# Latent heads in pairs on two column halves, differential scores as three fp32r products, and a unit's maximum ahead of the last unit's scaling

## What is computed

```python
def _softmax_attention(q, k, v, scale):          # layer 0: 8 heads, 64+32 wide keys, 64 wide values
    s = jnp.einsum('bhqd,bhkd->bhqk', qb, k).astype(jnp.float32) * scale
    p = jax.nn.softmax(s, axis=-1)
    return jnp.einsum('bhqk,bhkd->bhqd', p.astype(v.dtype), v)

def _diff_attention(q1, q2, k1, k2, v, lam, scale):   # layer 1: 8 heads, two 64 wide halves, 128 wide values
    p1 = jax.nn.softmax(jnp.einsum('bhqd,bhkd->bhqk', qa, k1).astype(jnp.float32) * scale, axis=-1)
    p2 = jax.nn.softmax(jnp.einsum('bhqd,bhkd->bhqk', qb, k2).astype(jnp.float32) * scale, axis=-1)
    return jnp.einsum('bhqk,bhkd->bhqd', (p1 - lam * p2).astype(v.dtype), v)
```

## Time and profile before

| | |
|---|---|
| median of 3 timed runs | 1863.83 us (1862.94 to 1865.37) |
| the profiled execution: its time, its span | 1864.37 us, 1862.6 us |
| busy share of the span | TensorE 81%, VectorE 40%, ScalarE 23%, GpSimd 11% |
| mean granted TensorE clock | 0.913 of full speed |

### The profile page before, as it was taken

The page is one execution under the profiler, slowest core; times in us unless marked ns, Lnnn a source line. Parts: engine busy times, 40 slices in busy tenths (PEclk is TensorE's granted clock), DMA queues, the critical chain, the costliest instruction groups (busy, mean ns, idle before and its releaser), DMA issues. The chain is left out here.

```text
span 1862.6 us, 25715 instructions
## 1 busy us (share of the span) xinstructions
PE 1517.4 (81%) x9767; PEld 1213.7 (65%) x9768; DVE 744.2 (40%) x1388; ACT 426.4 (23%) x832; POOL 214.2 (11%) x166
## 2 busy tenths in 40 slices
PE   4699999656899997599993199989997867999970
PEld 1588888555576444477882199987884446777760
DVE  0312122266477343311114835428993752111118
ACT  1311212242343011011112312125552111101113
POOL 1000000112000032100003400010000321100016
PEclk9899999878999998699997599999998977999995
DMA  7576755701000901559994032220006225877763
GB/s 270 176 238 211 242 182 160 171 12 31 1 1 1 296 34 54 170 173 342 354 352 168 23 94 69 80 60 1 1 1 183 102 91 198 280 260 256 269 215 146
DMA packets 190509, 277.82 MB, mean 149 GB/s; under 512 B 12888, under 2 KB 130352, under 8 KB 190416
## 3 DMA queue, kind: packets, MB, share of 16 engines
q1 hardware_dynamic: 180032, 239.15, 39.0%
q0 software_dynamic: 9520, 34.24, 5.3%
q10 hardware_dynamic: 864, 3.15, 0.4%
HBM read 246.90 MB, written 34.85 MB: 151 GB/s over the span
## 5 line engine op out<-in xcount | busy, mean ns | idle before, releaser
L480 PEld LDWEIGHTS psum<-in_parts 128*128 128x128 f32 x3360 | 411.3, 191 | 59.2 <-issue 59.2
L480 PE MATMUL psum<-in_parts 128*128 128x258 f32 (+1 forms) x3360 | 421.2, 286 | 25.3 <-PEq L322 25.3
L773 PE MATMUL psum<-layer 128*128 128x512 f32 x400 | 173.7, 594 | 2.7 <-PEq L698 2.7
L1777 PEld LDWEIGHTS psum<-layer 128*128 128x128 f32 x1280 | 145.7, 192 | 15.2 <-issue 7.6
L1777 PE MATMUL psum<-layer 128*128 128x128 f32 x1280 | 146.5, 275 | 6.7 <-DVE layer L1983 6.7
L1777 PEld LDWEIGHTS psum<-layer,arena 128*128 128x128 f32 x1152 | 137.9, 200 | 13.2 <-issue 6.7
L1777 PE MATMUL psum<-layer,arena 128*128 128x128 f32 x1152 | 138.6, 284 | 5.3 <-DVE layer L1983 3.6
L773 PEld LDWEIGHTS psum<-layer 128*128 128x128 f32 x400 | 75.8, 191 | 95.2 <-issue 95.2
L566 DVE COPY arena<-psum 128x258 f32<-128x258 f32 (+1 forms) x70 | 29.7, 425 | 240.8 <-PE psum L480 240.8
L1168 PE MATMUL psum<-layer 128*128 128x320 f32 (+1 forms) x384 | 114.2, 434 | 5.0 <-PEq L1358 1.7
L1265 ACT ACTIVATE layer<-psum,layer 128x640 f32<-128x640 f32 (+1 forms) x120 | 84.3, 705 | 118.5 <-DVE layer L1211 118.5
(11 more groups left out here) (298 smaller groups left out, 1872.7 us busy)
## 6 DMA issues: line engine op xcount, KB each, us to landing
arena<-in_moe_w SPq DMA_DIRECT2D x48, 1024.0 KB, 9.3
layer<-in_moe_w SPq DMA_DIRECT2D x48, 1024.0 KB, 8.7
in<-in_ada_w SPq DMA_DIRECT2D x40, 1024.0 KB, 5.2
y_rows<-layer SPq DMA_DIRECT2D x64, 256.0 KB, 8.5
in<-in_ev_w_in SPq DMA_DIRECT2D x15, 1032.0 KB, 7.6
in<-in_od_w_in SPq DMA_DIRECT2D x11, 1024.0 KB, 5.1
start<-in_ada_w SPq DMA_DIRECT2D x8, 1024.0 KB, 16.6
arena<-mod_rows SPq DMA_DIRECT2D x16, 512.0 KB, 7.7
```

The lines of the kernel that those rows point to most:

```text
L480: last = T.matmul(bank(g % W_BANKS)[:, 0:cw], a, b[:, k], start=(k == 0 and m == 0), stop=(k == KD - 1 and m == 2))
L773: last = T.matmul(bank(g % 4), feats[k][:, t * P:(t + 1) * P], wout[:, k, j * BANK:(j + 1) * BANK], start=(k == 0), stop=(k == kt - 1))
L1777: last = T.matmul(dst[:, (2 * f + m) * P:(2 * f + m + 1) * P], weights[m][:, k, f * P:(f + 1) * P], xT[:, k, :], start=(k == 0), stop=(k = ...
```

## The change

`heads_attention` is replaced by two functions. In both VectorE takes `top(u)` ahead of `mix(u - 1)`; the order of TensorE's and ScalarE's steps stays.

- `latent_heads`: `values` is done for two heads at once, in every second turn: for each of the five key tiles a product for the even head into PSUM rows 0 to 63 and one for the odd head into rows 64 to 127. The result of both is copied out at once. The transposed weights have four buffers for two. VectorE now copies two of the five transposed tiles, ScalarE three.
- `difference_heads`: each of the four fp32 score matmuls becomes three fp32r products over 64 rows of contraction, without the zero padding. ScalarE copies all five transposed tiles.
- `differential_attention`: the evacuation of every query and key item is done twice, ScalarE writing the rounded part and VectorE the remainder (of the PSUM value and the rounded part); the zero padding falls away.
- Buffers move (`MLA_OUT`, the heads' buffers behind the projection), and the upper part of SBUF is taken anew around the differential attention; GpSimd drains at the end of retention.

```diff
+        def latent_heads(units, qT, kT, value, e_buf, put, rsum, nmax, pT):
...
+            LONG, ND = sum(len(kt) > 1 for kt in tiles), 2
+            def pair_at(u):
+                return u % 2 == 1 and u >= 3
...
+                @block.tensor
...
+                    def values(p):
+                        pe.wait_ge(c_d, 2 * p + 2)
+                        pe.wait_ge(c_a, min(2 * p + 2, LONG))
+                        if p >= 2:
+                            pe.wait_ge(put_s, p - 1)
+                        out = bank(6 + p % 2)
+                        for n, kt in enumerate(tiles[2 * p]):
+                            for r in range(2):
+                                u = 2 * p + r
+                                last = T.matmul(out[MDV * r:MDV * (r + 1), 0:P], value(units[u][1], kt), pT[:, u % 4, n, :],
+                                                start=(n == 0), stop=(n == len(tiles[u]) - 1))
+                        last.then_inc(valued, 1)
+
+                    for u in range(U + 2):
+                        if u < U:
+                            score(u)
+                        if pair_at(u):
+                            values((u - 3) // 2)
+                        if 1 <= u <= U:
+                            turn(u - 1)
...
+                @block.vector
...
+                    for u in range(U + 2):
+                        if u < U:
+                            top(u)
+                        if 1 <= u <= U:
+                            mix(u - 1)
+                        if pair_at(u):
+                            out((u - 3) // 2)
+                        if 1 <= u <= U:
+                            copy_p(u - 1)
...
+        def difference_heads(units, qT, kT, value, e_buf, lamr, put, rsum, nmax, pT, squares):
...
+            PRODUCTS = ((0, 0), (0, 1), (1, 0))
...
+                    def score(u):
+                        t, h = units[u]
+                        for s in range(2):
+                            if u:
+                                pe.wait_ge(expd, 2 * u - 1 + s)
+                            for a in range(1 if t == 0 else 2):
+                                for m, (x, y) in enumerate(PRODUCTS):
+                                    out, k0, n = (view(s, 1), NT * P, P) if t == 0 else (view(s, NT)[:, a], a * HK, HK)
+                                    last = T.matmul(out, qT(t, h, s, x), kT(h, s, y, k0, n), start=(m == 0), stop=(m == 2))
+                            last.then_inc(scored, 1)
...
                 @block.vector
...
                     for u in range(U + 2):
+                        if u < U:
+                            top(u)
                         if 1 <= u <= U:
                             mix(u - 1)
-                        if u < U:
-                            top(u)
                         if u >= 2:
                             out(u - 2)
-                        if 1 <= u <= U:
-                            copy_p(u - 1)
...
+                        A.copy(pT[:, u % 2, 0:n], bank(4, 2)[:, 0:n * P].rearrange("p (n q) -> p n q", n=n)).then_inc(copied, 1)
...
         def differential_attention(pj):
-                    evac(dve, 1)
+                    for n, (kind, h) in enumerate(items):
+                        dve.wait_ge(ev_a, n + 1)
+                        src = bank(2 * (n % 4), 2)
+                        if kind == "k":
+                            V.tensor_tensor(kT[1][:, h, :], src[:, 0:NK * P], whole(kT[0][:, h, :]), ALU.subtract).then_inc(ev_d, 1)
+                        else:
+                            V.scalar_tensor_tensor(qT[1][:, h, :], src[:, 0:TOK], DIFF_SCALE, whole(qT[0][:, h, :]),
+                                                   ALU.mult, ALU.subtract).then_inc(ev_d, 1)
...
-                    evac(act, 0)
+                    for n, (kind, h) in enumerate(items):
+                        act.wait_ge(tr, n + 1)
+                        src = bank(2 * (n % 4), 2)
+                        if kind == "k":
+                            A.copy(kT[0][:, h, :], src[:, 0:NK * P]).then_inc(ev_a, 1)
+                        else:
+                            A.mul(qT[0][:, h, :], src[:, 0:TOK], DIFF_SCALE).then_inc(ev_a, 1)
```

More of the change, by code:

```diff
@@ L1124, in _ @@
                         norm(t)
[L1126 to L1134, removed]
+        def latent_heads(units, qT, kT, value, e_buf, put, rsum, nmax, pT):
+            scored, maxed, expd = sem("mla_scored"), sem("mla_maxed"), sem("mla_expd")
+            mixed = sem("mla_mixed")
+            turned, c_a, c_d, valued, put_s = (sem(f"mla_{n}") for n in ("turned", "ca", "cd", "valued", "put"))
             U = len(units)
             tiles = [[NT] if t == 0 else list(range(NT)) for t, _ in units]
+            LONG, ND = sum(len(kt) > 1 for kt in tiles), 2
             def view(b, nk):
@@ L1157, in score @@
                         t, h = units[u]
[L1158 to L1169, removed]
+                        if u >= 2:
+                            pe.wait_ge(expd, u - 1)
+                        if t == 0:
+                            T.matmul(view(u % 2, 1), qT(t, h), kT(h, NT * P, P), start=True, stop=True).then_inc(scored, 1)
+                        else:
+                            for a in range(2):
+                                last = T.matmul(view(u % 2, NT)[:, a], qT(t, h), kT(h, a * KEYS // 2, KEYS // 2), start=True, stop=True)
+                            last.then_inc(scored, 1)
                     def turn(u):
@@ L1218, in mix @@
                         dchain.join(dve)
[L1219 to L1228, removed]
@@ L1237, in out @@
+                        e1, e2 = weights(u, 0, nk), weights(u, 1, nk)
+                        V.scalar_tensor_tensor(e1, e2, r[:, 1:2], e1, ALU.mult, ALU.add).then_inc(mixed, 1)
                     def out(u):
                         dve.wait_ge(valued, u + 1)
[L1239 to L1242, removed]
+                        V.tensor_scalar(put(*units[u]), out_of(u), rsum[:, 1, 2 * u:2 * u + 1], None, ALU.mult).then_inc(put_s, 1)
@@ L1467, in differential_attention @@
             lam1 = small[:, 32:34]
[L1468 to L1481, removed]
-                        if who == 0:
-                            last = A.mul(dst, half, DIFF_SCALE)
-                        else:
-                            last = V.tensor_scalar(dst, half, DIFF_SCALE, None, ALU.mult)
-                    last.then_inc(done, 1)
+            items = [("q", h) for h in range(DH)] + [("k", h) for h in range(DH)]
             with nc.Block(no_gpsimd_drain=True) as block:
@@ L1497, in _ @@
                           pj[:, 0, 2 * D:3 * D].rearrange("p (h d) -> p h d", h=DH))
-                items = [("q", h) for h in range(DH)] + [("k", h) for h in range(DH)]
-                @block.gpsimd
-                def _(pool):
-                    for r in range(2):
-                        rows = slice(DDH * (1 - r), DDH * (2 - r))
-                        nc.gpsimd.memset(qT[rows, :, r, :], 0.0)
-                    pool.drain()
                 @block.vector
```

188 lines of the change are left out of this document (124 added, 64 removed).

## The result

The changed kernel takes 1918.32 us (median of 4, 1916.03 to 1921.55), the kernel before beside it 1864.07 us (median of 4, 1862.94 to 1865.37): 1.0293 times as long, 95% interval 1.0278 to 1.0308. The profiled executions have spans of 1918.5 and 1862.6 us, 55.9 us apart.

| stretch | before, us | after, us | difference |
|---|---|---|---|
| start to the last block of retention's scores | 437.8 | 435.3 | -2.5 |
| from there to the latent preparation | 19.8 | 23.4 | +3.6 |
| latent preparation | 38.1 | 38.8 | +0.7 |
| latent loop, to the output projection | 111.3 | 129.2 | +17.9 |
| to layer 1, and layer 1 to the differential stage | 640.4 | 639.2 | -1.1 |

What follows compares the result with a forecast made beforehand. TensorE was taken to bound both loops before the change. Latent +12.3, differential +27.9, evacuation +2.7 and short units +2 sum to +44.9 us on 1864.37, so 1909 us; range 1890 to 1934.

Steps and rivals of the forecast that it cites:

- The ring: Both loops: scores, maximum, scaling, transposes, next scores run one after another; latent 3.42 us against 3.01, differential 4.75 against 3.82.
- the second half's maximum: Differential turn: starts 2.00 us after the scores start, after all twelve products; the first half's lies under the second half's products.
- my 0.15 us apart: Differential scores: pitch of the twelve fp32r products of 320 columns, taken in proportion to columns; 0.12 us otherwise.
- my 0.09: Differential turn: gap in us between transposes and next scores, for 64 rows of contraction; bounds 0 and 0.17.
- Rival B: Latent values: the column halves don't overlap, the pair takes 2.48 us; +12.6, 1922 us; chance 0.12.
- Rival C: Differential scores: weight loads show in the 64-row form, 0.32 us a product; +61, 1970 us; chance 0.09.
- Rival E: Both loops: the ring doesn't close and TensorE's work is the bound, differential 3.45 us, latent 2.39; 1837 us; chance 0.08.
- Rival D: Both loops: the clock falls because TensorE now idles in each turn; chance 0.05.
- Short units: Short units of both loops: the same ring on one key tile, +2 us together, bounds 0 and +8.
- The drain after retention: End of retention: costs nothing, because the barrier there waits for VectorE anyway.
- Evacuation: Ahead of the differential loop: ScalarE and VectorE each handle all 16 items; +2.7 us, bounds +1.6 and +3.7.

Runs made afterwards that it cites:

- experiment 1: The changed kernel with VectorE's order put back in both loops, scaling of the last unit before the maximum: 1857.19 us, 0.9968 of the kernel before.
- experiment 2: The kernel before with only VectorE's order changed, the maximum ahead of the last unit's scaling: 1914.62 us, 1.0281 of the kernel before.
- experiment 5: The changed kernel with transposes, copies, values and outputs one turn later and a third buffer for the weights: 1843.16 us, 0.9898 of the kernel before.
- experiment 4: The changed kernel with both halves' score products on rows 0 to 63: 1956.15 us in one execution, with other tokens sent to the experts.
- experiment 3: The kernel before with one GpSimd drain added at the end of retention: 1864.39 us, 1.0009 of the kernel before.
- experiment 6: The kernel of experiment 5 with 24 unread transposes on TensorE ahead of the differential loop: 1845.71 us, 0.9913 of the kernel before.
- experiment 7: The kernel of experiment 5 with the latent loop's paired values and their output one turn later still: 1831.47 us, 0.9841 of the kernel before.

## Why the prediction was right, and where it was off

The forecast was 1909 us and the kernel takes 1918: slower, for the reason given, with +55.9 us of span against +44.9.

**The ring: right.** The latent period is 3.43 us (3.42 forecast), the differential one 4.73 (4.75). By periods the rings cost 30 x 0.42 + 30 x 0.91 = 39.9 us, against 40.2 forecast. Experiments 1 and 2 show the order to be the cause from both sides: taken out of the changed kernel the loss is gone, put into the old one it is there. Experiment 5 shows that it is the ring and not the order as such, for there VectorE has the new order and TensorE no longer stands behind it.

**Inside the differential turn two terms were off and cancelled; that they left the sum within 0.02 us is luck.** I let the second half's maximum start 2.00 us after the scores. The first starts after 1.18 us, and the two, back to back, are what the reciprocal stands behind: 2.65 us where I had 2.73. So it is not the twelfth product that sets this step but VectorE's second maximum, queued behind its first. The twelve products are faster than my 0.15 us apart because the two row halves overlap: twelve take 1.54 us on both halves and, in experiment 4, 2.02 us on one. There they come (2.02 - 0.16) / 12 = 0.155 us apart, so the rate taken from the earlier trace rows was right and the overlap was missing. From the transposes to the scores it is 0.69 us, not 0.64: a gap of 0.14, between my 0.09 and my upper bound of 0.17. The runs show how long the gap is and not what causes it.

**Rivals B and C: fallen.** Twenty value records on both column halves take 1.31 us, as ten on one half did, and TensorE still waits 0.33 us after them. Twelve products with twelve weight loads take 1.54 us, not 12 x 0.32 = 3.84: the loads are hidden, on one row half too (2.02 us in experiment 4). **Rival E: fallen for the changed kernel,** and my bound for it, 3.45 us a differential unit once the ring is open, needs more than the old order: experiment 1 has that order and gets 3.80, where VectorE and ScalarE form the next ring. The bound holds where the transposes move (3.34 us, experiment 5).

**The terms that were too small** make up the 11 us:
- *The clock at the loops' starts, for which the sum had nothing.* Rival D had it fall through both loops, for TensorE's idle time. Inside them it stays at 1.00, with TensorE idle for 28% and 25% of the time. It fell at their starts: before, the first units of both run at full speed, at 1.00 from 495 to 505 and from 1258 to 1280 us; after, the granted clock is 0.50 from about 500 to 513 and 1288 to 1301 us. TensorE after, at both places:

```profile
503.19 2.34 PE L1162 MATMUL psum<-layer 96*128 96x320 f32 x4
...
508.24 2.34 PE L1162 MATMUL psum<-layer 96*128 96x320 f32 x4
```
```profile
1289.57 2.74 PE L1300 MATMUL psum<-heads_parts 64*128 64x320 f32 x12 [1.21 <-ACT arena L1374]
...
1295.74 2.67 PE L1300 MATMUL psum<-heads_parts 64*128 64x320 f32 x12
```

  A latent turn takes 5.05 us there (503.19 to 508.24) in place of 3.43: the ring has TensorE's scores and transposes in it, and both take about twice as long (the scores 2.34 us for 1.24; from the transposes to the next scores it is 1.12 us, 502.07 to 503.19, for 0.61). The long units grew by 16.6 and 30.3 us; less the rings' 12.6 and 27.3 this leaves 4.0 and 3.0 us, **7.0 us** for the starts. That all of it is the clock is not separated: the second differential turn (6.17 us for 4.11) may hold some of the ring as well. At the latent start the low clock need not be the change's doing, for experiment 3, whose latent loop is the old one, has it too:

```profile
500.00:502.00 2.00, 1.51 (x7) 1.28 (x7) 1.36 (x3) 0.57 (x1) 0.00 (x0) 0.50 0.00 0
```

  There it comes in some kernels (experiments 1 to 4 and 6, and the changed kernel) and not in others (before, experiments 5 and 7). At the differential start, in one profiled execution of each, it falls in every kernel with the new products and evacuation (the changed one, experiments 1 and 4 to 7) and in none with the old ones; experiment 2, with the new order, keeps 1.00 there from 1278 to 1300 us. So the order alone does not bring it down. What does is open.
- *Short units:* +1.3 and +3.4, **4.7 us** where I had 2. A differential one takes 2.6 us at 0.50 (1448.42 to 1451.02) and 2.1 at full clock (1444.12 to 1446.22), against 1.885 before.
- *The drain after retention:* costed at nothing because the barrier waits for VectorE anyway. It does not wait for VectorE alone: **2.4 us**, by the rows of experiment 3 (VectorE idle 2.88 us at the barrier for 0.51).
- *Evacuation:* **+3.4** for +2.7. VectorE's steps after, in order:

```profile
1271.75 3.81 DVE L1610 SCALAR_TENSOR_TENSOR heads_parts<-psum,heads_parts 128x640 fp32r<-128x640 f32 x5 [0.86 <-ACT heads_parts L1628]
1275.80 0.82 DVE L1610 SCALAR_TENSOR_TENSOR heads_parts<-psum,heads_parts 128x640 fp32r<-128x640 f32 x1 [0.24 <-ACT heads_parts L1628]
...
1278.92 7.00 DVE L1608 TENSOR_TENSOR heads_parts<-psum,heads_parts 128x768 fp32r<-128x768 f32 x8 [0.16 <-ACT heads_parts L1626]
```

  Its own steps are a little cheaper than taken (0.76 us apart for 640 columns, 0.87 for 768, in place of 0.80 and 0.92). What I left out are four waits for ScalarE behind the first, 0.16 to 0.24 us each, and a later start: VectorE's first step comes 5.82 us after the first transposes (at 1265.93), where the forecast has 5.53 (1247.37 to 1252.90).

These four are 12.8 us more than I had. The rings are 0.3 less, and the preparation's +0.7 and the small differences elsewhere (-2.5, -1.1, +0.2, and +1.2 beside the drain) take off 1.5, which leaves the 11 us.

## What to carry to other kernels

Before an engine's order is changed, follow the waits of one turn through every engine's own program order: where the first instruction of a turn on one engine waits for the last of the same turn on another, that chain is the period, however idle the engines are, and a faster operation outside it gives nothing. Move the consumers along with the producer: the order with which the changed kernel lost 2.9% goes with a gain of 1.0% once transposes, copies and values come a turn later (experiment 5), and of 1.6% with the paired values later still (experiment 7). When one ring is opened, look for the next, here 3.80 us between VectorE and ScalarE, before promising the engine's own work as the bound.

## What the runs showed of the hardware that was not expected

- Products that contract over 64 rows overlap with those on the other 64 rows, though all six of one half were issued ahead of the other six: twelve of 320 columns in 1.54 us, against 2.02 us on the same rows (experiment 4).
- Two column halves at once cost next to nothing: twenty value records in the 1.31 us of ten.
- TensorE's granted clock can stay at 0.50 for some 13 us of a loop's start in which TensorE is busy for 9.6 to 9.9 us, while inside the same loops, with TensorE idle 25 to 28% of the time, it stays at 1.00. Filling the idle time ahead of the differential loop moved the fall by a unit, made it shorter and did not prevent it.
